# Three pairs of probabilities in flight in the latent attention of a two-layer hybrid transformer step

## The reference, cut to what matters

```
q = rope_tail(mla_q); k = [rope_tail(k of latents) ; k of cache]        # 96 wide
s = (q @ k^T) * 96**-0.5                    # latents: 512 + 128 = 640 keys
p = softmax(s)                              # context tokens: their own 128 keys
o = p @ v                                   # v is 64 wide
```

## Time and profile before

| | |
|---|---|
| median of three runs | 1739.01 us |
| the profiled execution's own time | 1741.36 us |
| its span, first to last instruction | 1739.1 us |
| PE busy | 1610.1 us, 93% |
| DVE busy | 949.3 us, 55% |
| ACT busy | 664.1 us, 38% |
| POOL busy | 148.3 us, 9% |
| mean granted PE clock | 0.966 |
| DMA | mean 92 GB/s |

### The profile page before, as it was taken

How to read it: one execution, slowest core, us unless ns; L and a number is a source line. 1 busy time by engine, 2 the same in 40 slices (tenths; PEclk the granted TensorE clock), 3 DMA queues, 4 the chain that set the end, 5 groups by cost and what they waited for, 6 DMA issues and landing times.

```text
span 1739.1 us, 28317 instructions
## 1 busy us (share of the span) xinstructions
PE 1610.1 (93%) x11686; PEld 1489.9 (86%) x11686; DVE 949.3 (55%) x1480; ACT 664.1 (38%) x1045; POOL 148.3 (9%) x107
## 2 busy tenths in 40 slices
PE   5878897899999999999988799978999999999998
PEld 3755895589999999999967569946999999999998
DVE  3653346856555545654584433497566456554553
ACT  4554533753422322232244454357433222332231
POOL 1002102520000000000010030064000000000000
PEclk9898998999999999999999899989999999999999
DMA  9440443311222222223534205341222222222211
GB/s 312 156 144 1 72 142 103 112 47 52 76 94 70 69 81 73 73 73 116 191 106 135 85 1 119 106 155 50 73 74 73 73 73 73 73 73 73 91 55 61
DMA packets 150856, 160.14 MB, mean 92 GB/s; under 512 B 16390, under 2 KB 132808, under 8 KB 150728
## 3 DMA queue, kind: packets, MB, share of 16 engines
q1 hardware_dynamic: 150024, 158.13, 29.7%
q10 hardware_dynamic: 576, 0.16, 0.0%
q0 software_dynamic: 128, 0.05, 0.0%
HBM read 153.41 MB, written 4.65 MB: 91 GB/s over the span
## 4 chain that ended last, share of the span: by engine, by line
PE 78%; DVE 11%; ACT 6%; issue 3%; DMA 1%; ACTq 0%; DVEq 0%; SPq 0%
PE ps L1552 33%; PE ps L1895 26%; PE ps L1645 10%; PE ps L1617 2%; PE ps L1669 2%; PE ps L1532 1%; DVE extrema L1306 1%; PE ps L1578 1%; ACT pt_c L788 1%; DVE extrema L1289 1%; PE ps L1722 1%; PE ps L1700 1%; DMA ada_own<-in_w_ada 1%; DVE mod L1147 1%; DVE w_lo L1134 1%
## 5 line engine op out<-in xcount | busy, mean ns | idle before, releaser
L788 ACT ACTIVATE w_hi<-w_raw 128x2048 fp32r<-128x2048 f32 (+1 forms) x90 | 169.9, 1887 | 333.8 <-PE ps L1552 324.3
L1348 DVE SCALAR_TENSOR_TENSOR xT<-ps,mod,xT 128x128 f32<-128x128 f32 (+2 forms) x432 | 190.0, 440 | 195.8 <-PE ps L1552 183.9
L1134 DVE TENSOR_TENSOR w_lo<-w_raw,w_hi 128x2048 fp32r<-128x2048 f32 (+1 forms) x90 | 203.1, 2257 | 140.4 <-ACT w_hi L788 138.9
L1895 PE MATMUL ps<-xa_hi,w_hi 128*128 128x320 f32 (+1 forms) x1024 | 236.1, 312 | 0.0
L1895 PE MATMUL ps<-xa_lo,w_hi 128*128 128x320 f32 (+1 forms) x1024 | 235.2, 311 | 0.0
L1895 PE MATMUL ps<-xa_hi,w_lo 128*128 128x320 f32 (+1 forms) x1024 | 235.1, 311 | 0.0
L1552 PE MATMUL ps<-z_hi,w_hi 128*128 128x320 f32 x1024 | 233.7, 310 | 0.9 <-DVE xT L1348 0.9
L1552 PE MATMUL ps<-z_lo,w_hi 128*128 128x320 f32 x1024 | 233.4, 309 | 0.0
L1552 PE MATMUL ps<-z_hi,w_lo 128*128 128x320 f32 x1024 | 233.3, 309 | 0.0
L1106 ACT ACTIVATE z_relu<-z_relu,sink_shift 128x128 f32<-128x128 f32 (+1 forms) x128 | 72.2, 564 | 307.0 <-DVE z_relu L1452 304.9
L1895 PEld LDWEIGHTS ps<-xa_hi,w_hi 128*128 128x128 f32 x1024 | 173.5, 189 | 0.3
(11 more groups left out here) (241 smaller groups left out, 2364.4 us busy)
## 6 DMA issues: line engine op xcount, KB each, us to landing
w_raw<-in_mlp_w SPq DMA_DIRECT2D x64, 1024.0 KB, 5.2
ada_own<-in_w_ada SPq DMA_DIRECT2D x54, 512.0 KB, 4.5
w_raw<-in_w_in SPq DMA_DIRECT2D x14, 1024.0 KB, 7.8
ada_mix<-in_w_ada SPq DMA_DIRECT2D x21, 512.0 KB, 7.8
ada_room<-in_w_ada SPq DMA_DIRECT2D x15, 512.0 KB, 8.9
w_raw<-in_w_out SPq DMA_DIRECT2D x8, 768.0 KB, 5.3
ada_first<-in_w_ada SPq DMA_DIRECT2D x6, 512.0 KB, 9.1
x_in<-in_x_sample SPq DMA_DIRECT2D x1, 2048.0 KB, 8.6
```

What stands on the lines that cost most here:

```text
L788: do(nc.scalar.activation(out, in_, ACT.Copy), sem)
L1134: do(V.tensor_tensor(w_lo[:, n % 2, 0:w], w_raw[:, n % 2, 0:w], f32(w_hi[:, n % 2, 0:w]), ALU.subtract), w_lo_ready)
L1348: do(V.scalar_tensor_tensor(dst, src, gate[:, m:m + 1], dst, ALU.mult, ALU.add), sem if last else None)
L1895: last = M.matmul(bank(b + a_, s1 - s0), w[r][:, k, c:c + P], x[:, k, s0:s1], start=k == 0 and q == 0, stop=k == KC - 1 and q == 2)
```

## The change

`pr_c` becomes three places, two at the old addresses and a third in space that the stage's earlier buffers have left. Place `i % 3` holds pair i. The lag of C becomes 3 in all three loops: PE turns pair j-3 behind the score of pair j and multiplies the values of pair j-4, ACT's `exps(j)` waits for `turned(j-3)`, and its copy and rounding, like DVE's `take_out`, are one pair later. The two projected tiles move from steps 10 and 11 to steps 11 and 12. The turned probabilities keep two places and the scores one.

```
--- before.py
+++ after.py
@@ -275,7 +275,7 @@
     sq_cq = at("sq_cq", T0 + 2080, [P, NT, Q_RANK])
     sq_up = at("sq_up", T0 + 4384, [P, (NT + 1) * 4 * QK])
     rope_tmp_c = at("rope_tmp_c", T0 + 8480, [P, 2, 4, 4, ROPE])
-    pr_c = at("pr_c", T0, [P, 2, 2, NT * P])
+    pr_c = [at(f"pr_c{i}", T0 + off, [P, 2, NT * P]) for i, off in enumerate((0, 1280, 7680))]
     pt_c = at("pt_c", T0 + 2560, [P, 2, 2, NT * P])
 
     a_q = at("a_q", A0, [P, 2, NTOK])
@@ -475,7 +475,7 @@
 
         def probs(i, pair):
             kind, b, _ = pair
-            return (pr_c[:, i % 2] if kind == "C" else pr_a[i % 3])[:, :, 0:keys_of(kind, b) * P]
+            return ((pr_c if kind == "C" else pr_a)[i % 3])[:, :, 0:keys_of(kind, b) * P]
 
         def probs_t(i, pair):
             kind, b, _ = pair
@@ -488,7 +488,7 @@
             eng.wait_ge(ada_dma[ada_place(u)], 16 * (len(ada_before(u)) + 1))
 
         IN_ATTENTION = 20
-        LAG = {"C": 2, "AD": 3}
+        LAG = 3
 
         def late_ticks(l, stage):
 
@@ -912,16 +912,15 @@
                     copy(d_k[:, :], trans_view(i, NTOK + PAST), t_act)
 
             def attention(l, kind_list):
-                lag = LAG[kind_list]
+                lag = LAG
                 todo = [(pair_at[(l, *p)], p) for kind in kind_list for p in attention_pairs(kind)]
 
                 def exps(i, pair):
                     kind = pair[0]
                     act.wait_ge(max_ready, signals(i, 0))
-                    ring = LAG["C" if kind == "C" else "AD"]
-                    if i >= ring:
-
-                        act.wait_ge(turned, i - ring + 1)
+                    if i >= LAG:
+
+                        act.wait_ge(turned, i - LAG + 1)
                     scale = SCALE_C if kind == "C" else SCALE
                     if kind == "D":
 
@@ -1796,7 +1795,7 @@
                     pe.wait_ge(exp_done, signals(pair_at[(l, "C", 3, 1)], 0))
                     project(l, U + 3, "naq", range(t, t + 1))
 
-                attention(l, "C", {10: lambda: more_naq(2), 11: lambda: more_naq(3)})
+                attention(l, "C", {11: lambda: more_naq(2), 12: lambda: more_naq(3)})
                 project(l, U + 3, "naq", range(4, NT))
                 project(l, U + 4, "nak")
                 pe.wait_ge(pt_ready, did["pair"])
```

## The result

The changed kernel takes 1747.2 us in the median of eight runs (1743.04 to 1754.71), the kernel before 1737.97 us beside it (1734.14 to 1741.87): a ratio of 1.006, with a 95% interval of 1.0044 to 1.0076, or 8 to 13 us more. By the medians it is 9.2 us. The forecast was 1747.4 us and +8.4. The profiled execution, with 1743.04 us and a span of 1741.0, is the fastest of the eight; its span is only 1.9 us above that of the profiled execution of before (1739.1), and the first lesson is why.

What follows compares the result with a forecast made beforehand. The prediction took a 5.44 us loop through ACT and DVE as the bound; 5.0 + 1.7 - 2.5 = 4.2 us a layer, twice, gave +8.4 on 1739.01: 1747.4 us, range 1739.5 to 1754.0.

Steps and rivals of the forecast that it cites:

- What bounds the stage: In C's attention, a loop through ACT and DVE sets the step at 5.44 us, with PE outside it.
- settled steps: Steps from 6 on in C's attention, released by DVE's maximum: they stay at 5.44 us, no cost or gain.
- the buffer was the bound: Rival, chance 0.06: steps 5 to 9 shrink from 5.45 to 4.95 us; 1733.8 us in all.
- The start, 2.5 us a layer: First steps of C's attention: ACT's exponentials no longer wait for the place in `pr_c`; 2.5 us gained a layer.
- The end, 5.0 us: After score 9, PE idles before `turn(7)`, and turn and values come ahead of tile 2: 5.0 us lost a layer.
- the clock behind it, 1.7 us: After PE's idle time in step 10, 3.4 us of work at half speed: 1.7 us lost a layer.
- hole of 2.9 us: Step 10: PE stands idle 2.9 us before `turn(7)`, which waits for ACT's copy of pair 6.
- The sum: Per layer 5.0 + 1.7 - 2.5 = 4.2 us, twice for two layers: +8.4 us, 1747.4 us.
- clock better: Rival, chance 0.12: clock returns before score 4 and also holds at the end; +1.2 us, 1740.2 us.
- clock worse: Rival, chance 0.18: clock returns a step later at the start, stays low for two stretches at the end; 1754.6 us.
- held behind a hole of 2.92 us: Rival, chance 0.20: the clock holds behind PE's idle time, without the 1.7 us; +5.0, 1744.0 us.
- The repeating gap as a sign of missing buffers: Skill's rule: PE's gap of 0.50 us a step would be closed by a third buffer; the forecast held otherwise.

Runs made afterwards that it cites:

- d1: The changed kernel with DVE's `take_out` behind both maxima of the step in C's attention instead of ahead of them: 1743.19 us, ratio 1.0034 to the kernel before.
- g1: The changed kernel with the tiles at steps 10 and 11 and DVE's `take_out` between the two heads' maxima: 1736.84 us, ratio 1.0000 to the kernel before.
- f1: The kernel before with three places (lag 2, tiles at 10 and 11 kept) and `take_out` between the two heads' maxima: 1728.22 us, ratio 0.9945.
- p1: The kernel before with three places for the probabilities, lag 2 and tiles at steps 10 and 11 kept: 1732.88 us, ratio 0.9978.
- p2: One more profile of the kernel before with three places and lag 2 kept: 1730.42 us, a single execution.
- h1: The changed kernel with 20 transposes of the identity, read by nobody, ahead of `turn(7)`: 1749.37 us, ratio 1.0063 to the kernel before.
- m1: The kernel before, two places and lag 2 kept, with only the two projected tiles moved to steps 11 and 12: 1742.41 us, ratio 1.0037.
- a1: The changed kernel run again, unaltered, beside other experiments: 1747.8 us, ratio 1.0063 to the kernel before.
- t1: The changed kernel with the two projected tiles back at steps 10 and 11, lag 3 kept: 1738.85 us, ratio 1.0013 to the kernel before.

## Why the prediction was right, step by step

**What bounds the stage.** Right. The settled steps kept 5.45 us and their 1.76 us wait for DVE, and opening the loop on DVE's side shortened them to 5.27 (d1), 4.87 (g1) and 4.69 us (f1). The rival by which the buffer was the bound fell with that: three places alone leave them at 5.45 (p1). One reading was off: PE's 4.95 us of busy time were taken for the least that a step can have, and f1 runs at 4.69. The rival's price, 2.5 us a layer, was set too low by that.

**The start, 2.5 us a layer.** The mechanism was right in the main (the place ends the waits of pairs 2 and 3), the number the middle of a range. At equal time at 0.5 the change gains 44.25 - 40.97 = 3.3 us (17 us low) and about 39.6 - 37.6 = 2.0 us (6.8 us low). The forecast held the clock's stretch fixed by the first profile of before, 17 us in both layers; that was the longest of the three profiles of that kernel, and the clock is not the same from one execution to the next. Under its own condition, 17 us at 0.5, the 2.5 is 0.8 too small. And it put the gain down to the place, while part of it is work that the lag moves behind the last score (p1 and p2). With lag 3 the exponentials of pairs 3 to 5 still wait for a turn; with lag 2 they don't.

**The end, 5.0 us, and the clock behind it, 1.7 us.** Right, and the larger part of the result. The tail is 30.79 to 31.11 us against 24.37, 6.4 to 6.7 us more, where 6.7 were forecast. Without the low clock it is 29.41 and 29.67 (h1), 5.0 to 5.3 us more. The clock's share is 1.4 us there by difference and 1.56 us in m1. That a hole of 2.9 us always costs it is not so: m1's second layer had none, while all six holes in the changed kernel's three profiles had one, and so had d1's hole of 1.78 us in one layer of two.

**The sum.** 6.5 - 2.0 or - 3.3 is 3.2 to 4.5 us a layer, 6 to 9 us in all; the times say 8 to 13. The forecast of 8.4 is inside, at the lower end. What was missing in the sum is more time at half speed in the kernel as a whole: by the mean granted clocks some 10 us beyond the holes, worth an estimated 2.5 us, which would make it 8.5 to 11.5. Part of it may lie in the heads. With lag 3 they have 14.8 us at 0.5 on average in fourteen (with d1's 10.2 and 17.1 and g1's 8.4 and 25.2), with lag 2 9.2 us in fourteen (with f1's 7.8 and 8.3). With so few draws that is not shown, and what makes the stretches longer stays open. That the forecast of 1747.4 us lies 0.2 from the median is luck: it stood on 1739.01 for before, which measured 1737.97 beside the change, a start that gains more and a low clock that costs more than forecast made up for each other.

**The rivals.** The three clock cases are not rivals to the rest but other draws of it, and a part of each was met. The clock was back before score 4, as in *clock better*, in the first profile of the change (141.4); it stayed low longer at the start than forecast, as in *clock worse*, in a1 (until 159.3 in the first layer); and it held behind a hole of 2.92 us only in m1's second layer, never in the changed kernel. That the tiles were free to move, a rival that t1 and m1 were built to test, fell with them. The repeating gap as a sign of missing buffers (the Trainium skill, Perfetto Trace Analysis, Optimization Strategy) was not borne out in the settled steps; it was in steps 2 and 3, where ACT's wait named the turn that frees its place.

## What to carry to other kernels

A deeper buffer and a longer lag are two changes, and they should be tried apart. Here the buffer paid best where the consumer ran fewer steps behind than there were places; when both grew together, the wait for the place stayed in the same step (g1), and the further step of lag left one more pair's work behind the last score (t1). When a pipeline is lengthened, look at what stood in its drain as filler: it has to stay at the first step without a producer, or the drain starts with a hole, and on PE a clock at half speed may follow it (it did behind seven of the eight holes of 2.9 to 3.2 us read here). And when the stage is full of waits, find the loop that sets the step before adding depth: here the place of one subtraction of 0.29 us in DVE's step was worth 0.75 us a step (5.44 to 4.69). And two single profiles say little when the clock differs between them; compare stretches at the same time at 0.5, or parts that the clock leaves alone.

## What the runs showed of the hardware that was not expected

The granted clock's low stretches come and go between executions of one and the same program: the head of C's attention had 17.1, 9.0 and 7.7 us at 0.5 in the first layer of three profiles of the kernel before, with heads of 44.27, 40.22 and 39.68 us. And it came back late although PE was busy: in h1 and a1 it stayed at 0.5 for 23.9 us in the first layer, through a block of 9.31 us of scores that ran back to back. What in PE's work brings it back sooner was not found.
